# Decoder trunk on one core: the residual waits in DRAM during the experts, each pass adds its rows there, and the end works block by block

## The chip, the cores and the metric

The kernel runs on one core of a Trainium2 chip. TensorE (PE in the profile) multiplies, VectorE (DVE), ScalarE (ACT) and GpSimd (POOL) do the elementwise work, and SyncE (SP) issues most transfers. The metric is the device time of one execution in microseconds, as the median of several runs.

## The reference

Two layers over 256 tokens of width 2048, all in fp32. Each layer adds the output of an attention mixer to the residual h, and then that of a channel mixer: a dense SwiGLU in layer 0, and in layer 1 an expert SwiGLU in which each token goes to 2 of 8 experts. A final RMSNorm gives the output.

```python
h = x
for layer in range(2):
    h = h + hybrid_mixer(rmsnorm(h, attn_norm[layer]), ...)
    m = rmsnorm(h, ffn_norm[layer])
    if layer == 0:
        h = h + swiglu(m, dense_w_gate, dense_w_up, dense_w_down)
    else:
        y = 0
        for e in range(8):                       # gates are zero but for a token's top 2
            y = y + gates[:, e:e + 1] * swiglu(m, wg[e], wu[e], wd[e])
        h = h + y
return rmsnorm(h, final_norm)
```

## The kernel before

The tokens are two blocks of 128 (`BLOCKS`), which lie on the partitions; h is one tile of 128 x 2 x 2048 in on-chip memory. The 2048 columns are handled as four column blocks of 512 (`COLS`, `NCOL`). Each engine has its own program; they meet at semaphores. Weights stream through tiles of 1 MB (`raw`, `more_raw`: eight slots in the experts, issued by SP in `load` when the slot's last reader is done). A tile is two units. For each unit ACT writes the rounded part `w_hi` (`split_hi`), DVE the rest `w_lo` (`split_lo`, in the attention and dense parts one unit in four by POOL in `low_parts`), and PE multiplies hi by hi, lo by hi and hi by lo. ACT and DVE run three units ahead of PE (`LEAD`).

The experts run as passes: one pass is one expert with up to 128 of its tokens, 48 units (16 for the first half of gate and up, 16 for the second, 16 for the down product from `DOWN0` on). With these inputs there are 8 passes, of which 7 are trips of a hardware loop and the last one is written out behind it (`tail=True`). The steps around the change:

- Before the experts, DVE writes the normed token rows in four column blocks (`gained`, semaphore `n_ready`), and POOL stores them to `tokens_dram` (`rows_out`). POOL first fills spare rows of the DRAM tensor `slots_dram`, waits for that (`spare_in`), and prepares `count`, `token` and the cleared tile `x_rows`.
- PE, DVE and ACT route the tokens; DVE writes the token number of each of the 128 slots of a pass into `slot_token` (`read_slots`, `slot_ready`). POOL then gathers these rows into `x_rows`, which is the tile scr (`gather_rows`, one indirect DMA; slots without a token have a number beyond the bound and move nothing). PE transposes the rows (`turn_rows`), and the pass starts.
- In a pass ACT copies the four column blocks of the down product to `y_out` (`down_end`), and POOL stores them in three DMAs to the pass's rows of `slots_dram` (`store_y`).
- After the loop POOL gathers, for both blocks and both experts of a token, the rows of `slots_dram` at `home`, and adds them into h on the way (four indirect DMAs). It starts when a late weight tile has landed.
- The last pass's rows never go to DRAM: PE brings them back to token order with a 0/1 matrix (`put_rows`, at the units of `put_at` and once behind the pass), and DVE adds them to h (`add_back`).
- The end: DVE multiplies by the final gain (`gain_back`), ACT squares h with a row sum (`square_back`), `one_over_rms` makes the scale, DVE scales block 0 and ACT block 1, and SP stores the output.

## Time and profile before

| what | value |
|---|---|
| median of 3 runs | 2269.82 us (2269.7 to 2271.07) |
| profiled execution: span from first to last instruction | 2270.2 us |
| PE busy | 2222.1 us, 98% |
| DVE busy | 1565.4 us, 69% |
| ACT busy | 1240.7 us, 55% |
| POOL busy | 376.8 us, 17% |
| read from and written to DRAM | 515.10 MB, 15.75 MB |

The span is the only time that the profiled execution has; it lies within the range of the three runs. PE's busy time says only that matmuls follow each other closely. Times in the rows below count from the start of this span, and the experts' passes run from about 1690 to 2252.

### The profile page before, as it was taken

The page shows a single profiled execution, that of the slowest core. Times are in us where ns is not written, and L with a number is a line of the kernel's source. Part 1 is how long each engine was busy: PE and PEld are TensorE (multiplying, and loading weights), DVE is VectorE, ACT ScalarE, POOL GpSimd, SP SyncE. Part 2 cuts the span into 40 slices and gives each one's busy share as a digit, 9 for nine tenths or more (in the row PEclk, how much of TensorE's full clock was granted, in tenths as well). Part 3 has the DMA queues.
Part 4 walks back from the last instruction along what each step waited for, and adds up shares of the span by engine and source line. Part 5 has one row for each costly group of instructions (what it writes and reads, how often), then busy time and mean ns, then how long its engine had stood idle before and what let it go on. Part 6 is the DMA issues. An engine that isn't in the chain of part 4 may idle for free. (4 is left out here: it accounts for less than half of the span.)

```text
span 2270.2 us, 29218 instructions
## 1 busy us (share of the span) xinstructions
PE 2222.1 (98%) x10255; PEld 1827.3 (80%) x10255; DVE 1565.4 (69%) x1716; ACT 1240.7 (55%) x1531; POOL 376.8 (17%) x196
## 2 busy tenths in 40 slices
PE   7999999999999999999999999999999999999997
PEld 6888888888888888888877888888877888888875
DVE  4466686666655566665554466686679999999997
ACT  5445454454444344444435445454458888887885
POOL 1111221222222222222212121121210000000001
PEclk9999999999999999999999999999999999999998
DMA  7464545555565565656554454555599999999997
GB/s 245 149 191 156 185 157 190 183 172 193 180 198 186 187 200 186 193 180 198 185 177 159 153 193 149 185 173 193 185 341 349 382 383 382 381 380 374 381 383 203
DMA packets 264462, 523.43 MB, mean 231 GB/s; under 512 B 15237, under 2 KB 19465, under 8 KB 263177
## 3 DMA queue, kind: packets, MB, share of 16 engines
q1 hardware_dynamic: 259648, 500.42, 65.0%
q0 software_dynamic: 4544, 22.03, 3.0%
q8 instruction: 45, 0.74, 0.1%
q14 instruction: 25, 0.20, 0.0%
q10 hardware_dynamic: 200, 0.05, 0.0%
HBM read 515.10 MB, written 15.75 MB: 234 GB/s over the span
## 5 line engine op out<-in xcount | busy, mean ns | idle before, releaser
L660 ACT ACTIVATE w_hi<-raw 128x1024 fp32r<-128x1024 f32 x744 | 778.6, 1058 | 609.0 <-PE acc L1575 558.1
L999 DVE TENSOR_TENSOR w_lo<-raw,w_hi 128x1024 fp32r<-128x1024 f32 x606 | 758.1, 1270 | 477.1 <-ACT w_hi L660 474.9
L1573 PE MATMUL acc<-w_hi,a_hi 128*128 128x512 f32 x1632 | 644.2, 395 | 3.9 <-DVE w_lo L999 2.4
L1575 PE MATMUL acc<-w_hi,a_lo 128*128 128x512 f32 x1632 | 637.0, 390 | 0.0
L1574 PE MATMUL acc<-w_lo,a_hi 128*128 128x512 f32 x1632 | 636.6, 390 | 0.0
L572 POOL TENSOR_TENSOR w_lo<-raw,w_hi 128x1024 fp32r<-128x1024 f32 x138 | 337.8, 2447 | 1304.7 <-ACT w_hi L660 1005.2
L1573 PEld LDWEIGHTS acc<-w_hi,a_hi 128*128 128x128 f32 x1632 | 307.3, 188 | 67.7 <-DVE w_lo L999 3.8
L1575 PEld LDWEIGHTS acc<-w_hi,a_lo 128*128 128x128 f32 x1632 | 307.0, 188 | 65.1
L1574 PEld LDWEIGHTS acc<-w_lo,a_hi 128*128 128x128 f32 x1632 | 307.2, 188 | 61.4
L1866 PE MATMUL acc<-w_hi,a_hi 128*128 128x512 f32 x752 | 300.5, 400 | 4.2 <-DVE w_lo L999 4.1
L1868 PE MATMUL acc<-w_hi,a_lo 128*128 128x512 f32 x752 | 293.6, 390 | 0.0
L1867 PE MATMUL acc<-w_lo,a_hi 128*128 128x512 f32 x752 | 292.9, 389 | 0.0
L999 DVE TENSOR_TENSOR w_lo<-more_raw,w_hi 128x1024 fp32r<-128x1024 f32 x192 | 231.1, 1222 | 30.3 <-ACT w_hi L660 26.7
L1573 PE MATMUL acc<-w_hi,o_hi 128*128 128x512 f32 x608 | 240.5, 396 | 2.4 <-DVE o_lo L1282 2.4
L1575 PE MATMUL acc<-w_hi,o_lo 128*128 128x512 f32 x608 | 237.6, 391 | 0.0
L1574 PE MATMUL acc<-w_lo,o_hi 128*128 128x512 f32 x608 | 237.3, 390 | 0.0
L660 ACT ACTIVATE w_hi<-more_raw 128x1024 fp32r<-128x1024 f32 x192 | 197.5, 1054 | 21.6 <-PE acc L1868 18.0
L1866 PEld LDWEIGHTS acc<-w_hi,a_hi 128*128 128x128 f32 x752 | 141.3, 188 | 37.0 <-DVE w_lo L999 9.3
L1868 PEld LDWEIGHTS acc<-w_hi,a_lo 128*128 128x128 f32 x752 | 141.1, 188 | 30.6
L1867 PEld LDWEIGHTS acc<-w_lo,a_hi 128*128 128x128 f32 x752 | 141.4, 188 | 28.3 <-issue 0.7
L1573 PEld LDWEIGHTS acc<-w_hi,o_hi 128*128 128x128 f32 x608 | 114.6, 189 | 26.4 <-DVE o_lo L1282 2.6
L1575 PEld LDWEIGHTS acc<-w_hi,o_lo 128*128 128x128 f32 x608 | 114.6, 188 | 24.3
(237 smaller groups left out, 1497.0 us busy)
## 6 DMA issues: line engine op xcount, KB each, us to landing
raw<-in_w_in SPq DMA_DIRECT2D x112, 1024.0 KB, 5.0
raw<-in_moe_w_gate SPq DMA_DIRECT2D x64, 1024.0 KB, 10.0
more_raw<-in_moe_w_up SPq DMA_DIRECT2D x64, 1024.0 KB, 10.3
raw<-in_dense_w_gate SPq DMA_DIRECT2D x44, 1024.0 KB, 5.2
raw<-in_dense_w_up SPq DMA_DIRECT2D x44, 1024.0 KB, 5.2
raw<-in_dense_w_down SPq DMA_DIRECT2D x44, 1024.0 KB, 5.2
raw<-in_w_out SPq DMA_DIRECT2D x32, 1024.0 KB, 5.2
raw<-in_moe_w_down SPq DMA_DIRECT2D x32, 1024.0 KB, 8.2
```

Source lines behind the costliest of these rows:

```text
L572: nc.gpsimd.tensor_tensor(w_lo[:, u % SPLIT_SLOTS], raw[:, (u // TILE_UNITS) % RAW_SLOTS, u % TILE_UNITS], w_hi[:, u % SPLIT_SLOTS].bitcas ...
L660: nc.scalar.activation(w_hi[:, slot], raw_tile(tile)[1][:, u % TILE_UNITS], ACT.Copy)\
L999: nc.vector.tensor_tensor(w_lo[:, slot], raw_tile(u // TILE_UNITS)[1][:, u % TILE_UNITS], w_hi[:, slot].bitcast(F32), ALU.subtract).then_i ...
L1573: nc.tensor.matmul(dst, hi, w_hi[:, slot, c], start=first and c == 0, stop=False)
L1574: nc.tensor.matmul(dst, hi, w_lo[:, slot, c], start=False, stop=False)
L1575: ins = nc.tensor.matmul(dst, lo, w_hi[:, slot, c], start=False, stop=last and c == UNIT_CHUNKS - 1)
L1866: nc.tensor.matmul(dst, hi, w_hi[:, slot, c], start=first and c == 0, stop=False)
L1867: nc.tensor.matmul(dst, hi, w_lo[:, slot, c], start=False, stop=False)
L1868: ins = nc.tensor.matmul(dst, lo, w_hi[:, slot, c], start=False, stop=last and c == UNIT_CHUNKS - 1)
```

## The change

The residual itself is put into DRAM for the time of the experts. POOL no longer fills spare rows; behind each store of a token column block it stores the same columns of h to a new tensor `h_dram` (semaphore `h_out`). In a pass, one indirect DMA (`add_rows`) takes the place of the three stores: it adds the 128 rows of `y_out` to the rows of `h_dram` that `slot_dest` names, where slots without a token again move nothing. `slot_dest` is a copy of `slot_token` that DVE makes right before `read_slots` overwrites it, behind a wait for the add of the pass before. The four gathers after the loop and the four small DVE operations that made `home` are gone; SP loads h back in four plain DMAs, one for each column block, behind its last weight load. The end is rearranged: `put_rows` runs two units earlier for column block 1 and one unit earlier for block 2, DVE squares three of the pieces itself, adds the last column block in two halves, and folds the final gain into the scaling, so that five pieces of the output leave one after the other.

```diff
-    put_at = {DOWN0 + 9: 0, DOWN0 + 13: 1, PASS_UNITS - 1: 2}
+    put_at = {DOWN0 + 9: 0, DOWN0 + 11: 1, PASS_UNITS - 2: 2}
...
 
                     after_first(e, passes - 1)
-
-            for n, half in enumerate((slice(0, D // 2), slice(D // 2, D))):
-                for b, scaled in enumerate((r_ready, s_ready)):
-                    sp_.wait_ge(scaled, 1 + n)
-                    sp_.dma_start(out[0, b * P:(b + 1) * P, half], h_gained[:, b, half]).then_inc(stored, 16)
-            sp_.wait_ge(stored, 16 * 2 * BLOCKS)
+                    sp_.wait_ge(rows_out, lin(16 * (NCOL - 1), 16, passes))
+                    for c in range(NCOL):
+                        sp_.dma_start(h[:, :, c * COLS:(c + 1) * COLS],
+                                      h_dram[:, c * COLS:(c + 1) * COLS].rearrange("(b p) n -> p b n", p=P))\
+                            .then_inc(returned[c], 16)
+
+            for b, cols, scaled, n in OUT_PIECES:
+                sp_.wait_ge(s_ready if scaled == "act" else r_ready, n)
+                sp_.dma_start(out[0, b * P:(b + 1) * P, cols], h_gained[:, b, cols]).then_inc(stored, 16)
+            sp_.wait_ge(stored, 16 * len(OUT_PIECES))
 
 
...
-            spare = slice((EXPERTS - 1) * P, MAX_PASSES * P)
-            pool.dma_start(slots_dram[spare, :], moe_w_down[0, 0][0:(MAX_PASSES - EXPERTS + 1) * P, :]).then_inc(spare_in, 16)
-            pool.wait_ge(consts, N_CONSTS)
-            pool.dma_start(slots_dram[NO_SLOT:NO_SLOT + 1, :].rearrange("o (a n) -> (o a) n", n=P), fx_neg[0:CH, P:2 * P])\
-                .then_inc(spare_in, 16)
             pool.wait_ge(w_ready, 8 * DEPTH)
-            pool.wait_ge(spare_in, 32)
             nc.gpsimd.iota(count, pattern=[[1, P]], base=0, channel_multiplier=0,
...
@@ -593,6 +591,8 @@
                 pool.wait_ge(n_ready, q + 1)
                 pool.dma_start(tokens_dram[:, q * COLS:(q + 1) * COLS].rearrange("(b p) n -> p b n", p=P), n_rows[q])\
                     .then_inc(rows_out, 16)
+                pool.dma_start(h_dram[:, q * COLS:(q + 1) * COLS].rearrange("(b p) n -> p b n", p=P),
+                               h[:, :, q * COLS:(q + 1) * COLS]).then_inc(h_out, 16)
...
-            def y_done(jobs_, i):
+            def add_rows(i):
 
                 for s in range(2):
-                    pool.wait_ge(free[s], lin(ffn_uses[1] + jobs_[s], 4, i))
+                    pool.wait_ge(free[s], lin(ffn_uses[1] + 4, 4, i))
+                pool.wait_ge(dest_ready, lin(1, 1, i))
                 pool.sem_inc(transfer_may, 1)
-
-            def store_y(n, i, done):
-                pool.dma_start(slots_dram[bass.ds(i * P, P), Y_COLS[n]], y_out[:, Y_COLS[n]]).then_inc(done, 16)
+                pool.indirect_dma_start(h_dram[:], bass.IndirectOffsetOnAxis(slot_dest[:, 0:1], 0), y_out, None,
+                                        bounds_check=BLOCKS * P - 1, oob_is_err=False, compute_op=ALU.add)\
+                    .then_inc(rows_out, 16)
 
             gather_rows(0)
+            pool.wait_ge(h_out, 16 * NCOL)
             pool.wait_ge(table_ready, 1)
             passes = pool.value_load(table[0:1, TABLE:TABLE + 1], min_val=EXPERTS, max_val=MAX_PASSES)
             with pool.Fori(0, passes - 1) as i:
                 gather_rows(1, 1, i)
-                y_done((3, 3), i)
-                store_y(0, i, rows_out)
-                y_done((4, 3), i)
-                store_y(1, i, rows_out)
-                y_done((4, 4), i)
-                store_y(2, i, rows_out)
-            last = passes - 1
-
-            pool.wait_ge(back_ready, 1)
-            pool.wait_ge(rows_out, last * 48 + 16 * NCOL)
-
-            tile_loaded(pool, M0 // TILE_UNITS + PASS_TILES - 4, PASS_UNITS, last)
-            pool.sem_inc(transfer_may, 1)
-            for j in range(2):
-                for b in range(BLOCKS):
-                    if j:
-                        pool.wait_ge(returned[b], 16)
-                    pool.indirect_dma_start(h[:, b, :], None, slots_dram[:],
-                                            bass.IndirectOffsetOnAxis(home[:, 2 * j + b:2 * j + b + 1], 0),
-                                            compute_op=ALU.add).then_inc(returned[b], 16)
+                add_rows(i)
...
-            for c in range(NCOL):
-                square_back(c)
+            square_back(0, range(BLOCKS), 0)
+            square_back(1, range(BLOCKS), 1)
+            square_back(NCOL - 1, (1,), 2)
             norm_guess(4)
             act.wait_ge(rr_ready, 5)
-            act.wait_ge(fin_gained, NCOL)
-            for half in (slice(0, D // 2), slice(D // 2, D)):
-                nc.scalar.activation(h_gained[:, 1, half], h_gained[:, 1, half], ACT.Copy, scale=rr[:, 1:2])\
-                  .then_inc(s_ready, 1)
+            act.wait_ge(fin_gained, 1)
+            nc.scalar.activation(h_gained[:, 1, 0:2 * COLS], h_gained[:, 1, 0:2 * COLS], ACT.Copy, scale=rr[:, 1:2])\
+              .then_inc(s_ready, 1)
...
-                    dve.wait_ge(sq_cols, NCOL * n)
+                    dve.wait_ge(sq_cols, NCOL * n if n < 4 else NCOL * 3 + 3)
+                    if n == 4:
+                        dve.wait_ge(squared_own, 3)
...
-            def add_back(c):
-
-                if c == 0:
-                    for b in range(BLOCKS):
-                        dve.wait_ge(returned[b], 32)
-                dve.wait_ge(put_ps, c + 1)
-                cols = slice(c * COLS, (c + 1) * COLS)
-                nc.vector.tensor_tensor(h[:, :, cols], h[:, :, cols], put_to[c], ALU.add).then_inc(h_added, 1)
-
-            def gain_back(c):
-
-                if c == 0:
-                    dve.wait_ge(fin_in, 32)
+            def add_back(c, blocks):
+
+                if blocks[0] == 0:
+                    dve.wait_ge(returned[c], 16)
+                dve.wait_ge(put_ps, c + 1 if len(blocks) == BLOCKS else c + 1 + blocks[0])
+                cols, b0, b1 = slice(c * COLS, (c + 1) * COLS), blocks[0], blocks[-1] + 1
+                nc.vector.tensor_tensor(h[:, b0:b1, cols], h[:, b0:b1, cols], put_to[c][:, b0:b1], ALU.add)\
+                  .then_inc(h_added, 1)
+
+            def square_own(c, b, to):
+
                 dve.wait_ge(h_added, c + 1)
-                cols = slice(c * COLS, (c + 1) * COLS)
-                gain_out = fin[c // 2][:, c % 2 * COLS:(c % 2 + 1) * COLS]
-                nc.vector.tensor_tensor(h_gained[:, :, cols], h[:, :, cols],
-                                        gain_out.rearrange("p (o n) -> p o n", o=1).broadcast_to([P, BLOCKS, COLS]),
-                                        ALU.mult).then_inc(fin_gained, 1)
+                nc.vector.scalar_tensor_tensor(out=to, in0=h[:, b, c * COLS:(c + 1) * COLS], scalar=1.0,
+                                               in1=h[:, b, c * COLS:(c + 1) * COLS], op0=ALU.mult, op1=ALU.mult,
+                                               accum_out=sums[:, b, c:c + 1]).then_inc(squared_own, 1)
+
+            def gain_back():
+
+                dve.wait_ge(fin_in, 32)
+                dve.wait_ge(h_added, 2)
+                nc.vector.tensor_tensor(h_gained[:, 1, 0:2 * COLS], h[:, 1, 0:2 * COLS], fin[0], ALU.mult)\
+                  .then_inc(fin_gained, 1)
...
                 if u == slots_read and not tail:
+                    dve.wait_ge(rows_out, lin(16 * NCOL, 16, i))
+                    nc.vector.tensor_copy(slot_dest[:], slot_token[:]).then_inc(dest_ready, 1)
+                    dve.wait_ge(dest_ready, lin(1, 1, i))
                     read_slots(1, 1, i)
...
-            for c in range(NCOL):
-                add_back(c)
-                gain_back(c)
+            both = range(BLOCKS)
+            add_back(0, both)
+            add_back(1, both)
+            gain_back()
+            add_back(2, both)
+            square_own(2, 0, scr[:, 2 * COLS:3 * COLS])
+            square_own(2, 1, scr[:, 3 * COLS:4 * COLS])
+            add_back(3, (0,))
+            add_back(3, (1,))
+            square_own(3, 0, eg[:, 0])
             one_over_rms(4)
-            dve.wait_ge(fin_gained, NCOL)
-            for half in (slice(0, D // 2), slice(D // 2, D)):
-                nc.vector.tensor_scalar(h_gained[:, 0, half], h_gained[:, 0, half], rr[:, 0:1], None, ALU.mult)\
-                  .then_inc(r_ready, 1)
+            for b, cols, scaled, n in OUT_PIECES:
+                if scaled == "dve":
+                    gain_out = fin[cols.start // (2 * COLS)]
+                    at = cols.start % (2 * COLS)
+                    nc.vector.scalar_tensor_tensor(out=h_gained[:, b, cols], in0=h[:, b, cols], scalar=rr[:, b:b + 1],
+                                                   in1=gain_out[:, at:at + cols.stop - cols.start], op0=ALU.mult,
+                                                   op1=ALU.mult).then_inc(r_ready, 1)
...
                 for b in range(BLOCKS):
                     ins = nc.tensor.matmul(put_to[c][:, b], pick_any[:, b], y_out[:, c * COLS:(c + 1) * COLS], start=True, stop=True)
-                ins.then_inc(put_ps, 1)
+                    if c == NCOL - 1 or b == BLOCKS - 1:
+                        ins.then_inc(put_ps, 1)
```

POOL, from its last `low_parts` to the end of its program. Before, the two fills of `slots_dram` come first, the token stores follow each other, a pass has three stores, and the four gathers into h stand at the end:

```order
L581 DMA slots_dram<-in_moe_w_down 64x16384
L583 DMA slots_dram<-fx_neg 16x128
L587 IOTA sp 128x128
...
L594 DMA tokens_dram<-nat 128x2x512 x2
L594 DMA tokens_dram<-qT 128x2x512
L594 DMA tokens_dram<-kT 128x2x512
L606 DMA scr<-tokens_dram,slot_token 128x2048
...
L606 DMA scr<-tokens_dram,slot_token 128x2048
...
L617 DMA slots_dram<-nat 128x1024
...
L641 DMA h<-slots_dram,home 128x2048 x4
L161 UNCONDITIONAL_BRANCH
```

And of the changed kernel, the same stretch:

```order
L585 IOTA sp 128x128
...
L592 DMA tokens_dram<-nat 128x2x512
L594 DMA h_dram<-h 128x2x512
...
L592 DMA tokens_dram<-kT 128x2x512
L594 DMA h_dram<-h 128x2x512
L606 DMA scr<-tokens_dram,slot_token 128x2048
...
L606 DMA scr<-tokens_dram,slot_token 128x2048
...
L616 DMA h_dram<-nat,slot_dest 256x2048
```

The iotas and the clearing of scr now stand behind `low_parts` alone, a store of h follows each of the four stores of tokens, and one indirect DMA per pass is left beside the gather.

DVE, from the last `w_lo` of the last pass on (h is the residual, X and acc are the accumulators that `put_rows` wrote, raw is `h_gained`, sm the small sums and scales). Before:

```order
L999 TENSOR_TENSOR w_lo<-more_raw,w_hi 128x1024
L1457 TENSOR_TENSOR h<-h,X 128x2x512
L1466 TENSOR_TENSOR raw<-h,qT 128x2x512
L1457 TENSOR_TENSOR h<-h,X 128x2x512
L1466 TENSOR_TENSOR raw<-h,qT 128x2x512
L1457 TENSOR_TENSOR h<-h,acc 128x2x512
L1466 TENSOR_TENSOR raw<-h,kT 128x2x512
L1457 TENSOR_TENSOR h<-h,acc 128x2x512
L1466 TENSOR_TENSOR raw<-h,kT 128x2x512
L1036 TENSOR_REDUCE sm<-sm 128x2
L1004 TENSOR_SCALAR sm<-sm 128x2
...
L1044 TENSOR_SCALAR sm<-sm 128x2
L1558 TENSOR_SCALAR raw<-raw,sm 128x1024 x2
```

And of the changed kernel:

```order
L982 TENSOR_TENSOR w_lo<-more_raw,w_hi 128x1024
L1432 TENSOR_TENSOR h<-h,X 128x2x512 x2
L1446 TENSOR_TENSOR raw<-h,qT 128x1024
L1432 TENSOR_TENSOR h<-h,acc 128x2x512
L1438 SCALAR_TENSOR_TENSOR scr,sm<-h 128x512 x2
L1432 TENSOR_TENSOR h<-h,acc 128x512 x2
L1438 SCALAR_TENSOR_TENSOR eg,sm<-h 128x512
L1021 TENSOR_REDUCE sm<-sm 128x2
...
L1029 TENSOR_SCALAR sm<-sm 128x2
L1549 SCALAR_TENSOR_TENSOR raw<-h,sm,qT 128x512 x2
L1549 SCALAR_TENSOR_TENSOR raw<-h,sm,kT 128x1024 x2
```

Ahead of the sum stood eight operations of 1024 elements; now there are four of 1024 and five of 512, and only the last three, two adds and a square, need the last `put_rows`. The scaling has grown from two operations to four.

PE, its last rows: the last products of the pass and the products with the 0/1 matrix (`nat,wT`, each "x2" one column block). Before:

```order
L1866 MATMUL acc<-w_hi,a_hi 128x512
L1867 MATMUL acc<-w_lo,a_hi 128x512
L1868 MATMUL acc<-w_hi,a_lo 128x512
L1866 MATMUL acc<-w_hi,a_hi 128x512
L1867 MATMUL acc<-w_lo,a_hi 128x512
L1868 MATMUL acc<-w_hi,a_lo 128x512
L1855 REGISTER_ALU
L1857 MATMUL acc<-nat,wT 128x512 x4
```

And of the changed kernel, where block 2 comes ahead of the last unit (the six products) instead of behind it:

```order
L1847 REGISTER_ALU
L1849 MATMUL acc<-nat,wT 128x512 x2
L377 REGISTER_ALU
L1859 MATMUL acc<-w_hi,a_hi 128x512
L1860 MATMUL acc<-w_lo,a_hi 128x512
L1861 MATMUL acc<-w_hi,a_lo 128x512
L1859 MATMUL acc<-w_hi,a_hi 128x512
L1860 MATMUL acc<-w_lo,a_hi 128x512
L1861 MATMUL acc<-w_hi,a_lo 128x512
L1849 MATMUL acc<-nat,wT 128x512 x2
```

## Rows read from the trace of the kernel before

**Rows 1.** Stretches; us, busy of PE, PEld, DVE, ACT, POOL, PEclk, DMA share, GB/s
```profile
1666.00:1676.00 10.00, 10.00 (x50) 8.32 (x51) 9.29 (x55) 3.66 (x6) 2.35 (x4) 1.00 1.05 408
...
1770.00:1840.00 70.00, 69.57 (x320) 56.88 (x319) 66.25 (x72) 57.02 (x65) 2.73 (x4) 1.00 1.05 384
```

**Rows 2.** Timeline of POOL from 1660 on
```profile
1663.31 0.27 POOL L587 IOTA sp<- 128x128 f32 x1 [15.58 <-DMA slots_dram<-fx_neg]
...
1667.62 0.73 POOL L594 DMA_DIRECT2D tokens_dram<-kT  x1
...
1736.69 1.06 POOL L606 DMA_INDIRECT scr<-tokens_dram,slot_token  x1 [54.76 <-DVE slot_token L1411]
```

**Rows 3.** DMA issues from 1660 to 1669, last number us to landing
```profile
tokens_dram<-kT POOLq DMA_DIRECT2D x1, 512.0 KB, 11.8
```

**Rows 4.** Timeline of DVE from 1636 to 1703
```profile
1658.57 1.22 DVE L1069 TENSOR_TENSOR kT<-h,nat 128x1024 f32<-128x1024 f32 x1
...
1673.09 0.15 DVE L1411 TENSOR_SCALAR slot_token<-X 128x1 uint32<-128x1 f32 x1
```

**Rows 5.** The rows gather, tile scr
```profile
L606 POOL DMA_INDIRECT scr<-tokens_dram,slot_token x8: 1058/1091/1594, 1680.3 to 2158.1; - x8
...
DMA to landing us min/median/max: 7.1/8.2/9.8
```

**Rows 6.** Timeline of PE and chain of waits, 1679 to 1703
```profile
1687.45 1.09 PE L1848 MATMUL X<-ident,scr 128*128 128x128 f32 x8 [3.48 <-DMA scr<-tokens_dram,slot_token]
...
1692.88 0.87 PE X L1848 x8
1693.76 0.23 PE acc L1866
```

**Rows 7.** Waits of PE from 1700 to 2250
```profile
PE X L1848 <- DMA scr<-tokens_dram,slot_token: 2.4, 3, 1.7
```

**Rows 8.** DMA issues of one pass, 1770 to 1840
```profile
more_raw<-in_moe_w_up SPq DMA_DIRECT2D x8, 1024.0 KB, 10.7
```

**Rows 9.** Timelines of SP and ACT: a weight tile issued, and read
```profile
2203.09 8.37 SPq L431 DMA_DIRECT2D raw<-in_moe_w_down  x4
...
2214.22 8.68 SPq L431 DMA_DIRECT2D more_raw<-in_moe_w_down  x4
...
2220.41 1.07 ACT L660 ACTIVATE w_hi<-raw 128x1024 fp32r<-128x1024 f32 x1 [0.18 <-PE acc L1868]
```

**Rows 10.** Timeline of POOL from 2195 on
```profile
2222.05 1.76 POOL L641 DMA_INDIRECT h<-slots_dram,home  x1 [40.45 <-DMA more_raw<-in_moe_w_down]
...
2240.56 2.57 POOL L641 DMA_INDIRECT h<-slots_dram,home  x1 [2.35 <-DMA h<-slots_dram,home]
```

**Rows 11.** DMA issues from 2221 to 2224
```profile
more_raw<-in_moe_w_down SPq DMA_DIRECT2D x1, 1024.0 KB, 16.7
```

**Rows 12.** Two stretches without weight loads; last number GB/s
```profile
2240.00:2242.00 2.00, 1.00 1.00 193
...
2266.00:2268.00 2.00, 0.50 1.02 403
```

**Rows 13.** Timeline of PE from 2236 on
```profile
2246.36 1.88 PE L1857 MATMUL X<-nat,wT 128*128 128x512 f32 x4
...
2250.85 3.59 PE L1857 MATMUL acc<-nat,wT 128*128 128x512 f32 x8
```

**Rows 14.** Timelines of DVE and ACT from 2250 on
```profile
2250.73 1.22 DVE L1457 TENSOR_TENSOR h<-h,X 128x1024 f32<-128x1024 f32 x1 [4.09 <-DMA h<-slots_dram,home]
...
2260.60 0.16 DVE L1036 TENSOR_REDUCE sm<-sm 128x2 f32<-128x8 f32 x1
...
2262.49 1.41 DVE L1558 TENSOR_SCALAR raw<-raw,sm 128x1024 f32<-128x1024 f32 x2
...
2251.05 0.60 ACT L950 ACTIVATE nat<-acc 128x512 f32<-128x512 f32 x1 [5.66 <-PE acc L1868]
...
2262.62 2.19 ACT L985 ACTIVATE raw<-raw,sm 128x1024 f32<-128x1024 f32 x2 [1.29 <-DVE sm L1044]
```

More of the change, by code:

```diff
@@ L341, in trunk @@
         rows_out = sem("rows_out")
-        spare_in = sem("spare_in")
+        h_out = sem("h_out")
+        dest_ready = sem("dest_ready")
         transfer_may = sem("transfer_may")
@@ L351, in trunk @@
         gate_picked = sem("gate_picked")
-        returned = [sem(f"returned{b}") for b in range(BLOCKS)]
+        returned = [sem(f"returned{c}") for c in range(NCOL)]
         put_ready = sem("put_ready")
         put_ps = sem("put_ps")
-        back_ready = sem("back_ready")
         fin_gained = sem("fin_gained")
+        squared_own = sem("squared_own")
         s_ready = sem("s_ready")
```

30 lines of the change are left out of this document (10 added, 20 removed).

## The prediction

> **What bounds the kernel now.** I read busy time by stretch first, then who waits in the stretches that the diff touches. In a stretch of one pass's length PE is busy 69.57 of 70 us at a granted clock of 1.00 [rows 1]; in the whole of the passes its only larger waits are three, 2.4 us together, for the gather of a pass's rows [rows 7]. So the passes are bound by PE, and the change leaves PE's work in them alone. DVE is close behind, busy 66.25 of 70, and the DMA engines show a share of 1.05 at 384 GB/s: nothing there has much room [rows 1].
>
> That leaves two seams. At the start of the experts, POOL sits idle for 15.58 us until its fill of the spare rows has landed, at 1663.31 [rows 2]; only then does it store the tokens, the last one from 1667.62 to 1668.35. That store lands 11.8 us after its issue [rows 3], at 1679.4, and the gather starts 0.9 later, at 1680.3 [rows 5]. PE waits 3.48 us for it, until 1687.45, and comes back at the low clock [rows 6]. At the end, DVE waits 4.09 us for the gathers into h, until 2250.73, then works to 2260.60 before the row sums are complete, and the last scaled piece is ACT's, done at 2262.62 + 2.19 = 2264.81 [rows 14]. The span ends at 2270.2, 5.4 us later.
>
> **The first seam.** The spare fill (512 rows of 8 KB, read and written) and the wait for it go. POOL is then free for each token column block as DVE delivers it; the last is ready at 1658.57 + 1.22 = 1659.8 [rows 4], so its store is out by 1660.5, 7.8 us earlier. Even if it takes 11.8 us again it lands at 1672.3, before DVE has written the slots, at 1673.09 + 0.15 = 1673.24 [rows 4]. Now the slots release the gather. With the same 0.9 us it starts at 1674.1, and with 8.2 us to landing (7.1 to 9.8) [rows 5] the rows are there at 1682.3, at worst at 1683.9. PE is ready for them at 1687.45 - 3.48 = 1683.97. So the wait of 3.5 us is gone.
>
> The low clock goes with it. From 1687.45 to 1692.88 PE does eight transposes and one unit of twelve matmuls, 5.43 us. At the full clock, as right behind it, the eight transposes take 0.87 and a matmul 0.23 [rows 6], together 0.87 + 12 x 0.227 = 3.6 us. The idle time cost another 1.8. Gain: 3.5 + 1.8 = 5.3 us. It is between 2.2 (rival below) and 5.4; I take 5.3, since the margins on the way are 0.9 us at the slots and 0 to 2.8 at the landing.
>
> What is added here hides: the four stores of h are 2.1 MB where 8.4 MB of fill traffic leaves, they are issued by an otherwise idle POOL (0.73 us each), and the only one who waits for `h_out` is POOL behind its first gather, with its next work 50 us away (the gather at 1736.69, [rows 2]). The clearing of scr moves to about 1647, beside DVE's split work. It could hold DVE up to 1.8 us once; no row shows that pair of operations. DVE works three units ahead of PE there, some 4 us, so I take nothing.
>
> **The passes, seven times.** Three stores of 1.05 MB together go, and one indirect add comes. It moves only slots with a token: 512 token-expert pairs over 8 passes are 64 rows, 0.52 MB. The nearest row is the gather with addition at the end, which runs alone at 193 GB/s with all engines busy (share 1.00) [rows 12]; plain transfers reach 403 [rows 12] and 408 [rows 1]. So an add holds the engines 0.52 / 0.193 = 2.7 us and the stores held them 1.05 / 0.403 = 2.6: no change. The room is also there: a pass still moves 25.2 MB of weights and 0.5 MB of rows, 25.7 / 0.408 = 63 us of some 70.2, which leaves 7.2 us for the add. Its completion is wanted 40 us later (by the copy of `slot_token` at `DOWN0`, and by ACT's first `y_out`), its issue needs only POOL.
>
> What it may do is to delay weight tiles. A tile issued at 2203.09 is read by ACT at 2220.41 [rows 9], 17.3 us later, and lands within 10.7 [rows 8]: 6.6 us to spare. The tile issued together with two full gathers with addition took 16.7 [rows 11]; with a quarter of their rows in flight I expect 12 to 13. The Trainium skill (DMA: Bandwidth & Descriptors, Queues, rings and completion order) says that a semaphore increment lands only after every earlier write of that DMA engine, across its queues, so a weight tile's signal would wait for the add's writes too. The 16.7 us agree with it; by that rule alone a tile could be as late as the add itself, which here, by the rows of the gathers, would be about 10 us and inside 17.3, so it gives no other sum.
>
> DVE makes one copy more, ahead of `slot_token`: 0.15 us like its neighbour [rows 4] and a wait on itself, 0.2 to 0.25. The gather starts later by that, and PE waits for the gather already in three passes of seven [rows 7]. Cost: between 0 and 7 x 0.25 = 1.8 us; I take 0.7, three passes in full.
>
> **The end.** PE first. From its product for column block 1 at 2246.36 to that for block 2 at 2250.85 lie two units [rows 13], 12 x 0.227 = 2.7 us, so one such product costs PE 1.8. Today block 2 stands behind the last unit and hides ACT's last copy. Moved ahead of it, it puts the last unit's end from 2250.85 to 2252.6. ACT's copy starts 0.2 later and takes 0.6 [rows 14]: 2253.4. The product of block 3 then gives its first half at 2254.4 and its second at 2255.3 (3.59 us for two such products, [rows 13]).
>
> DVE was free of weights at 2250.73 - 4.09 = 2246.6. The plain loads of h replace the four gathers (2222.05 to 2250.7, [rows 10]). SP issues them behind its last weight load, at 2214.22 + 8.68 = 2222.9 [rows 9]; with at most 3 MB of weights ahead, 5.2 MB at 384 GB/s are in by 2236.5, 10 us before DVE wants them. So DVE adds blocks 0 and 1, multiplies one gain and adds block 2 (1.22 us each, [rows 14]) and squares twice (0.7 each, half as many elements) by about 2252.9. The halves of block 3 are added at 2255.0 and 2256.0, the last square ends at 2256.6. ACT squares two column blocks behind its copy (four halves of 0.67, estimated from its 0.60 copy and the read of the sum) and the last half, to 2256.9. The sums are complete at 2256.9, not 2260.60: 3.7 us earlier.
>
> The scale takes 2262.49 - 2260.60 = 1.9 us [rows 14]: 2258.8. Behind it DVE needs four two-input operations, 0.6 + 0.6 + 1.15 + 1.2 = 3.6, to 2262.4 where ACT ended at 2264.81: of the 3.7 us only 2.4 are left. The output is 2.1 MB at 403 GB/s [rows 12], 5.2 us, which before had to leave almost whole behind 2264. Now 0.8 MB can leave from 2260.2 on. If the last piece still needs 5.4 us, the gain stays 2.4; if it finds the engines free, it needs some 3.5 and the gain is 4.3. I take 4.6 for it: 2267.0, gain 3.2.
>
> **Sum.** -5.3 + 0.7 - 3.2 = -7.8, from 2270.2 to 2262.4. The median of the runs is 0.4 below the profiled span, so 2262.0.
>
> **Rivals.**
> - *The token stores stay late.* If the last one lands after 1674.8 (1683.97 - 8.2 - 0.9), PE waits again and meets the low clock. For it: each store now has a store of h in the same queue ahead of it, and weight loads run beside. Against: the fill's 8.4 MB are gone and the stores are spread over 15 us. If a third more traffic makes it 15.6 us, it lands at 1676.1: 1.3 of wait and 1.8 of clock come back, 2265.1. 12 in 100.
> - *The adds overrun the DMA engines: slower.* The add into DRAM has no row. It must read and write DRAM for each row. The 7.2 us of room hold up to 0.52 MB at 72 GB/s; each us above costs seven. At 8.3 us per add, three times my price, the gain is gone; at 9.7 the passes give 7 x 2.5 = 17.5 us back: 2279.5. PE would wait for w_lo, and w_lo for tiles. For it: 384 of 408 GB/s used, 16.7 us for a tile beside gathers. Against: 193 GB/s with addition. 12 in 100.
> - *The end does not move.* DVE's last scaling and the output remain the bound: with block 3 late by 1.8 us and squares that take longer than priced, the last piece leaves at 2264.5. 2265.0. 10 in 100.
> - *The change does not reach PE at all* (the gather late in every pass by what the seam gives). Against: the gather's price moves by 0.25 us at most. 3 in 100, near 2270.
>
> **Chances.** The forecast has 63 in 100, with its own range from 2258.5 to 2265. A change of 0.2%, 4.5 us, is about what a measurement of this kernel can tell: faster is below 2265.3. That takes the forecast and part of the first and third rival, 0.70. The rest of those and the last are the same, 0.17. Slower is 0.13. The range from 2258 to 2268 holds the forecast and the mild rivals, and leaves out the overrun.
>
> **What would show it.** Right: no wait of POOL before its iotas, a gather issued near 1674, no wait of 3.5 us on PE and no low clock near 1690; passes of the same length; h loaded before 2240; the row sums complete some 4.3 us behind PE's last unit (2252.6 to 2256.9), where it was 9.8 (2250.85 to 2260.60). Wrong: PE waits on w_lo within the first third of a pass (adds too slow), waits for the gather beyond 1 us in most passes, or an output that still takes 5.4 us behind the last scaling.

## The result, and the profile after

The changed kernel takes 2275.22 us (median of 16 runs, 2273.96 to 2276.05), the kernel before 2270.47 beside it (16 runs, 2267.45 to 2273.34): 1.002 times as long, 95% interval 1.0014 to 1.0027. It is slower by 0.2%, where I forecast 2262.0 and a range of 2258 to 2268. The profiled execution has a span of 2272.6 us and a time of 2274.41. All profiled executions behind this one have 1.6 to 1.8 us around their span too, so my "0.4 below the profiled span" was not a fixed distance, but an accident of which execution was profiled. That explains 2.2 us at most, and not the miss.

The first thing to compare is where the two traces part. The last piece of work that neither the diff nor its waits touch is POOL's last split, just ahead of its iotas. The timeline of POOL from 1640 on, of the kernel before (start us, duration):

```profile
1644.10 2.39 POOL L572 TENSOR_TENSOR w_lo<-raw,w_hi 128x1024 fp32r<-128x1024 f32 x1 [9.32 <-ACT w_hi L660]
```

And of the changed kernel, with what POOL does until the first gather:

```profile
1654.20 2.40 POOL L576 TENSOR_TENSOR w_lo<-raw,w_hi 128x1024 fp32r<-128x1024 f32 x1 [9.57 <-ACT w_hi L643]
1656.55 0.24 POOL L585 IOTA sp<- 128x128 f32 x1
...
1658.58 0.96 POOL L592 DMA_DIRECT2D tokens_dram<-nat  x1
1659.54 0.77 POOL L594 DMA_DIRECT2D h_dram<-h  x1
...
1670.19 0.72 POOL L592 DMA_DIRECT2D tokens_dram<-kT  x1 [4.66 <-DVE kT L1054]
...
1684.18 1.10 POOL L606 DMA_INDIRECT scr<-tokens_dram,slot_token  x1 [12.55 <-DVE slot_token L1396]
1741.82 1.10 POOL L606 DMA_INDIRECT scr<-tokens_dram,slot_token  x1 [56.53 <-DVE slot_token L1396]
```

The changed kernel is 10.1 us late before its first changed instruction runs. Read against that row, everything behind it went well: the iotas no longer wait ([rows 2] had 15.58 us of idle time), the gather is released by `slot_token` and no longer by the stores of tokens, and the waits of PE from 1640 to 1700 hold no gather (3.48 us in [rows 6]); the second gather is the first one in the loop.

The late part shows in PE. Groups of PE between 500 and 1160, inside layer 0's dense part, where the diff changes nothing (busy us, mean ns of one). The kernel before:

```profile
L1574 PE MATMUL acc<-w_lo,a_hi 128*128 128x512 f32 x637 | 247.8, 389 | 0.0
...
L1573 PE MATMUL acc<-w_hi,o_hi 128*128 128x512 f32 x320 | 124.5, 389 | 0.0
```

The changed kernel, same stretch:

```profile
L1566 PE MATMUL acc<-w_lo,a_hi 128*128 128x512 f32 x628 | 244.3, 389 | 0.0
L1565 PE MATMUL acc<-w_hi,o_hi 128*128 128x512 f32 x320 | 126.4, 395 | 0.0
```

The same product of the same shape takes 389 ns where the tile a_hi is its 128x128 operand, and 395 where it is o_hi. Before, both took 389. The page has 608 products with o_hi on each of the three lines, 1824 in all, and PE's busy time on it rose by 10.0 us, from 2222.1 to 2232.1.

The rest of the profile after, by the stages of the prediction. Waits of PE from 1700 on (total, times, longest):

```profile
PE acc L1859 <- DVE w_lo L982: 4.1, 10, 0.8
PE X L1840 <- DMA scr<-tokens_dram,slot_token: 2.5, 7, 0.4
PE acc L1849 <- ACT nat L933: 0.7, 1, 0.7
```

DMA issues from 1700 to 2230 (last number: median us to landing), the adds among them:

```profile
more_raw<-in_moe_w_up SPq DMA_DIRECT2D x59, 1024.0 KB, 13.5
...
h_dram<-nat,slot_dest POOLq DMA_INDIRECT x7, 12.0
```

The passes wait for the gather as much as before (2.5 us against the 2.4 of [rows 7]), only in seven small pieces. A weight tile now needs 13.5 us to land, in the same view of the kernel before 10.2; the prediction had 12 to 13, and PE's waits for w_lo did not grow with it. The end, timelines of SP, PE and DVE:

```profile
2232.80 6.46 SPq L539 DMA_DIRECT2D h<-h_dram  x4
...
2265.48 3.39 SPq L545 DMA_DIRECT2D out<-raw  x5
...
2245.03 1.88 PE L1849 MATMUL X<-nat,wT 128*128 128x512 f32 x4
...
2252.44 2.34 DVE L1432 TENSOR_TENSOR h<-h,X 128x1024 f32<-128x1024 f32 x2
...
2262.82 0.16 DVE L1021 TENSOR_REDUCE sm<-sm 128x2 f32<-128x8 f32 x1 [0.18 <-ACT scr L893]
...
2266.04 2.47 DVE L1549 SCALAR_TENSOR_TENSOR raw<-h,sm,kT 128x1024 f32<-128x1024 f32 x2
```

DVE no longer waits for h (4.09 us in [rows 14]). Since whole executions differ by more than these steps, I cut each trace at three rows that all kernels have: POOL's last split, the second gather of rows (the first one in the loop), and PE's first product that brings the last pass's rows back (`put_rows(0)`). In the changed kernel these rows stand above, in the kernel before they are at 1644.10, 1736.69 [rows 2] and, by PE's timeline:

```profile
2239.16 1.88 PE L1857 MATMUL X<-nat,wT 128*128 128x512 f32 x4
```

What lies between:

| us between | before | after | predicted change | change |
|---|---|---|---|---|
| start and POOL's last split | 1644.10 | 1654.20 | 0 | +10.1 |
| that and the second gather (first seam) | 92.59 | 87.62 | -5.3 | -5.0 |
| that and `put_rows(0)` (passes) | 502.47 | 503.21 | +0.7 | +0.7 |
| that and the end of the span | 31.04 | 27.57 | -3.2 | -3.5 |

The three steps that the change makes add up to -7.7, against -7.8 predicted. A fourth one, for which the sum had no term, is larger than all of them. How firm each row is, the other kernels of this case tell: the new end takes 27.6 or 27.7 us in every trace with it, but the passes scatter by about 2 us, so their +0.7 cannot be told from nothing.

### The profile page after: what moved, and what is told of

It reads as the page before. It is cut to its first block, busy times and chain, and to the rows that moved or that the text cites. A ratio compares the mean times of both kernels' runs of the same rounds, so it can differ in the third digit from the quotient of the medians.

```text
span 2272.6 us, 29186 instructions
## 1 busy us (share of the span) xinstructions
PE 2232.1 (98%) x10255; PEld 1825.0 (80%) x10255; DVE 1565.0 (69%) x1725; ACT 1238.2 (54%) x1524; POOL 375.3 (17%) x180
## 4 chain that ended last, share of the span: by engine, by line
PE 78%; DVE 10%; issue 5%; ACT 4%; DMA 3%; ACTq 0%; DVEq 0%; POOLq 0%; SPq 0%
PE acc L1565 20%; PE acc L1567 20%; PE acc L1566 20%; PE acc L1859 4%; PE acc L1861 4%; PE acc L1860 4%; DVE w_lo L982 3%; DMA scr<-tokens_dram,slot_token 3%; ACT w_hi L643 2%; PE X L1840 1%; PE X L1673 1%; DVE sm L987 1%; DVE nat L1125 1%; PE X L1593 0%; DVE eg L1469 0%
## 5 line engine op out<-in xcount | busy, mean ns | idle before, releaser
L643 ACT ACTIVATE w_hi<-raw 128x1024 fp32r<-128x1024 f32 x744 | 778.6, 1058 | 617.9 <-PE acc L1567 566.9
L643 ACT ACTIVATE w_hi<-more_raw 128x1024 fp32r<-128x1024 f32 x192 | 198.3, 1058 | 22.4 <-PE acc L1861 18.8
## 6 DMA issues: line engine op xcount, KB each, us to landing
raw<-in_moe_w_gate SPq DMA_DIRECT2D x64, 1024.0 KB, 13.5
more_raw<-in_moe_w_up SPq DMA_DIRECT2D x64, 1024.0 KB, 13.5
```

What stands on the lines that cost most here:

```text
L643: nc.scalar.activation(w_hi[:, slot], raw_tile(tile)[1][:, u % TILE_UNITS], ACT.Copy)\
```

## The experiments

The theory: the small tiles in front of o_hi got smaller, so o_hi, o_lo and `more_raw` moved. Every tile gets its place in a partition by its order in the program, rounded up to 32 bytes. The declarations and sizes in the kernel give the distances between the tiles, and the compiled programs the addresses: `back_at` and `home` (32 bytes each) became `slot_dest` (32), and o_hi went from byte 194176 to 194144, from a multiple of 128 to one 32 bytes short of it, while a_hi, declared earlier, stayed at 98432. The rival: the loss has another cause (the program's code, the place of DRAM buffers, the run).

### The tiles moved back, in both directions

In the pieces of code below the comments are mine, and "..." stands for lines left out.

```diff
 slot_dest = sb("slot_dest", [P, 1], U32)
+pad = sb("pad", [P, 8])                    # 32 unused bytes: o_hi at 194176
```

> The changed kernel, with an unused tile of 8 floats a partition (32 bytes) behind slot_dest, so that o_hi, o_lo and more_raw stand again at a multiple of 64 bytes in a partition, as before the change. Placement theory: the 9.8 us that the changed kernel is behind at POOL's w_lo row near 1640 us are gone (w_lo again near 1644.1), the products with o_hi take 389 ns in the mean again and not 395, and the time is 2275.2 - 9.8 = 2265.4 us, 0.998 of the kernel before, within 2263 to 2268. Rival, the loss has another cause (the shorter program, where the compiler puts the buffers in DRAM, the run itself): nothing changes, 2275 us, 1.002.

Measured: 2265.07 us (6 runs), 0.997 of the kernel before (0.9958 to 0.9982). The counterpart is the kernel before with the same line behind `home` (o_hi at 194208, 32 bytes past a multiple of 128):

> The kernel before, with the same unused 32 bytes behind home, so that o_hi, o_lo and more_raw stand 32 bytes off a multiple of 64, and nothing else is changed. Placement theory: slower by what the changed kernel is behind at 1640 us, 9 to 11 us, so 2279 to 2282, 1.004 of the kernel before, and nearly all of it ahead of 1640 us. If it is more than 11, the tiles of more_raw cost in the experts too. Rival, another cause: 2270.5 us, 1.000.

Measured: 2282.14 (5 runs), 1.0044 (1.003 to 1.0058). One unused tile takes 2275.22 - 2265.07 = 10.15 us from the one kernel and puts 2282.14 - 2271.79 = 10.35 on the other (2271.79 is the kernel before on the same chip). The first difference is between two chips; on the chip of 2265.07 the two slow kernels of the next section take 2275.75 and 2275.74. The rival is out. The products with o_hi, 500 to 1160, in the changed kernel with its tiles back and in the kernel before with its tiles moved:

```profile
L1566 PE MATMUL acc<-w_hi,o_hi 128*128 128x512 f32 x320 | 124.5, 389 | 0.0
```

```profile
L1574 PE MATMUL acc<-w_hi,o_hi 128*128 128x512 f32 x320 | 126.5, 395 | 0.0
```

Timelines of POOL and PE with the tiles back in place, the three rows of the table:

```profile
1646.01 2.39 POOL L577 TENSOR_TENSOR w_lo<-raw,w_hi 128x1024 fp32r<-128x1024 f32 x1 [9.32 <-ACT w_hi L644]
...
1733.61 1.11 POOL L607 DMA_INDIRECT scr<-tokens_dram,slot_token  x1 [56.52 <-DVE slot_token L1397]
...
2236.20 1.88 PE L1850 MATMUL X<-nat,wT 128*128 128x512 f32 x4
```

And POOL's last split in the kernel before with its tiles moved:

```profile
1655.49 2.39 POOL L573 TENSOR_TENSOR w_lo<-raw,w_hi 128x1024 fp32r<-128x1024 f32 x1 [9.57 <-ACT w_hi L661]
```

Over all kernels here, this row starts between 1643.7 and 1646.2 with o_hi at a multiple of 128 and nothing else moved (six traces, mean 1645.1), and between 1654.2 and 1655.6 with o_hi off it (five traces, mean 1655.0). That is 10.0 us for the 1783 of the 1824 products with o_hi that lie ahead of this row, 5.6 ns each.

### Another address, and only the DMA target moved back

```diff
+pad = sb("pad", [P, 16])                   # behind slot_dest: o_hi at 194208
```

> The changed kernel, with 16 unused floats (64 bytes) behind slot_dest: o_hi stands at another address, but again 32 bytes off a multiple of 64. Placement theory by multiples of 64 bytes: 2275 us as the changed kernel, o_hi products at 395 ns. Rival, any other address or size would help: 2265 us.

```diff
 o_hi, o_lo = ...                           # stay at 194144 and 210528
+pad = sb("pad", [P, 8])                    # ahead of more_raw alone: at 194176
 more_raw = sb("more_raw", [P, MOE_SLOTS - RAW_SLOTS, TILE_UNITS, UNIT_CHUNKS, COLS])
```

> The changed kernel, with the unused 32 bytes between o_hi and more_raw: o_hi and o_lo stay 32 bytes off, but the tiles of more_raw, which DMAs write to in the experts, stand at a multiple of 64 again. Theory that the products with o_hi cost it: still 2275 us, w_lo near 1654 us. Rival, the transfers into more_raw cost it: 2265 us. A side question: a tile's median landing in the passes rose from 10 to 13.5 us; if the misplaced target does it, it is back near 10 here, and if the seven adds do it, it stays at 13.5.

Measured: 2275.75 (10 runs, 1.0017) and 2275.74 (10 runs, 1.0016). Both as slow as the changed kernel: it is neither the size of the hole nor the target of the weight transfers. A few small tiles (`table`, `ncT`) move with o_hi in all these kernels and were not moved by themselves; what points at PE's operand are the rows of the products with it: at 5.6 ns each, 1824 of them are the whole loss. The side question is answered too: the landing of a tile of w_up stays at 13.5 us, so the adds cause that.

### Which operand, and which multiple

Two kernels put 32 unused bytes ahead of a pair of large tiles and 32 behind it, with o_hi and the rest meant to stay in place (both keep the 32 bytes behind `slot_dest`, so they are measured against 2265):

```diff
+pad_a = sb("pad_a", [P, 8])                # the other kernel: ahead of w_hi
 a_hi = sb("a_hi", [P, CH, BLOCKS * P], F32R)
 a_lo = sb("a_lo", [P, CH, BLOCKS * P], F32R)
+pad_b = sb("pad_b", [P, 8])                # the other kernel: behind w_lo
```

> The changed kernel with o_hi, o_lo and more_raw at a multiple of 64 bytes, but a_hi and a_lo 32 bytes off it (unused 32 bytes ahead of them and behind them). The names a_hi and a_lo are the 128x128 operand of 7152 products (1632 and 752, three of each). Theory that a loaded operand 32 bytes off makes a product 5.4 to 6 ns longer, wherever it is: 39 to 43 us slower where TensorE sets the time, so near 2305, with these products at 395 ns and not 389. In the experts, where the transfers are close to the bound too, it may be less, down to 2292. Rival, something else of o_hi's place (its address as such, or more_raw's): 2265.

> The changed kernel with all loaded operands at a multiple of 64 bytes, but w_hi and w_lo, the 512 moving columns of each product, 32 bytes off it. Theory that only the loaded operand matters: 2265. Rival, the moving operand's rows matter too, and more, since four times as many columns pass: by 6 ns for each of 8976 products 54 us slower, 2319, or more. A third: VectorE, ScalarE and POOL, which write these tiles, become slower, which would show in their rows' means and in PE's waits for w_lo.

Measured: 2305.36 us (1.0142) with a_hi and a_lo moved, 2304.23 (1.014) with w_hi and w_lo moved. The first number looks like what the theory said, but the groups of PE in that kernel, 500 to 1160, say more:

```profile
L1569 PE MATMUL acc<-w_lo,a_hi 128*128 128x512 f32 x638 | 252.3, 395 | 0.0
L1568 PE MATMUL acc<-w_hi,o_hi 128*128 128x512 f32 x292 | 115.5, 396 | 0.0
```

o_hi is slow here as well. My two holes added up to 64 bytes, so o_hi stood at 194240: a multiple of 64, but not of 128 (and in the second kernel a_hi stood like that too). So both kernels tested two things at once, and that 2305 came out is partly luck. About 10 of the 40 us belong to o_hi; a_hi's part is about 30, where the theory had 39 to 43.

The trace says where the rest is. POOL's last split starts at 1680.86 in it, 35.8 us behind the mean of the kernels in place. Less 10.0 for o_hi, that is 25.8 us for the 4800 products with a_hi ahead of it, 5.4 ns each. From the second gather to `put_rows(0)` there are some 2060 more, but this stretch takes 507.82 us, only 5.2 more than with all tiles in place (502.59), 2.5 ns for each. In place, PE waits 2.7 us for `w_lo` and 2.3 for the gather in this stretch; with the longer products it waits for neither. So a slower product costs its full price ahead of the passes, where PE hardly waits, and about half of it in this stretch, where PE has waits to give up.

The last two kernels take the two things apart:

```diff
-pad = sb("pad", [P, 8])
+pad = sb("pad", [P, 24])                   # behind slot_dest: o_hi at 194240
```

```diff
+pad_a = sb("pad_a", [P, 8])
 w_hi = sb("w_hi", [P, SPLIT_SLOTS, UNIT_CHUNKS, COLS], F32R)
 w_lo = sb("w_lo", [P, SPLIT_SLOTS, UNIT_CHUNKS, COLS], F32R)
+pad_b = sb("pad_b", [P, 24])               # 128 bytes in all: a_hi, o_hi in place
```

> The changed kernel with 24 unused floats (96 bytes) behind slot_dest: o_hi and o_lo stand at a multiple of 64 bytes that is no multiple of 128, and all other large tiles are at multiples of 128 as before. In the two kernels with a_hi or w_hi moved, o_hi stood like this, and its products too took 396 ns. Theory that the loaded operand wants a multiple of 128 bytes: slow like the changed kernel, 2275, products with o_hi at 395 ns. Rival, 64 is enough, and o_hi was slow there for another reason: 2265, 389 ns.

> The changed kernel with w_hi and w_lo, the 512 moving columns, 32 bytes off a multiple of 128, and every other large tile, a_hi and o_hi among them, at a multiple of 128. The kernel with w_hi moved had a_hi and o_hi at 64 off, so it did not tell the two apart. Theory that only the loaded operand matters: 2265, all products at 389 ns. Rival, the moving operand wants it too: by 5.4 ns for each of 8976 products up to 48 us slower, 2304 to 2313, products at 395 ns or more.

Measured: 2276.51 (10 runs, 1.002) with o_hi 64 bytes off and all else in place, and 2310.84 (4 runs, 1.0177) with only w_hi and w_lo 32 bytes off. Groups of PE, 500 to 1160, of the kernel with o_hi 64 bytes off:

```profile
L1567 PE MATMUL acc<-w_lo,a_hi 128*128 128x512 f32 x628 | 244.4, 389 | 0.0
L1566 PE MATMUL acc<-w_hi,o_hi 128*128 128x512 f32 x319 | 126.2, 396 | 0.0
```

And of the kernel with only the moving columns off:

```profile
L1569 PE MATMUL acc<-w_lo,a_hi 128*128 128x512 f32 x639 | 253.2, 396 | 0.0
...
L1568 PE MATMUL acc<-w_hi,o_hi 128*128 128x512 f32 x288 | 114.2, 397 | 0.0
```

So 64 is not enough, which also corrects the word "multiple of 64" in my earlier expectations, and my theory that only the loaded operand matters falls. The loaded operand (32, 64 or 96 bytes past a multiple of 128) or the moving one (tested at 32 only) makes the product 6 to 8 ns longer in these rows; with both off it is not twice that (2304.23 against 2310.84). The third rival is out: the rows of `w_lo` and `w_hi` are within 4 ns of those in place, and PE's waits for `w_lo` do not grow.

### The steps of the prediction, one by one

These start from the changed kernel with its tiles back in place (2265.07 us, on another chip; the kernel before takes 2271.79 there and 2271.76 here), and are read by the stretches of the table above.

**The seam put back.** POOL's fill of spare rows and of the zero row, and the wait for it:

```diff
+pool.dma_start(spare_dram[0:(MAX_PASSES - EXPERTS + 1) * P, :], moe_w_down[0, 0][0:(MAX_PASSES - EXPERTS + 1) * P, :]).then_inc(spare_in, 16)
+pool.wait_ge(consts, N_CONSTS)
+pool.dma_start(spare_dram[SPARE_ROW:SPARE_ROW + 1, :].rearrange("o (a n) -> (o a) n", n=P), fx_neg[0:CH, P:2 * P])\
+    .then_inc(spare_in, 16)
 pool.wait_ge(w_ready, 8 * DEPTH)
+pool.wait_ge(spare_in, 32)
```

> The changed kernel with its tiles back in place (the unused 32 bytes of the first experiment), and POOL's old work ahead of the experts put back: the fill of spare rows and of a zero row in DRAM, and the wait for it, ahead of the iotas. Theory that the seam gave 4.7 to 5.3 us: 2265.1 + 5 = 2270, with PE's wait of about 3.5 us for the first gather back, and the low clock after it. If the gain came only from the wait in POOL's order and another wait now ends later, less: 2267. Rival, the seam gave nothing and the gain lies elsewhere: 2265.

Measured: 2275.17 us (10 runs, 1.0015), twice the loss that I expected. Its waits of PE, 1640 to 1700, and its DMA issues, 1648 to 1675:

```profile
PE X L1849 <- DMA scr<-tokens_dram,slot_token: 8.0, 1, 8.0
```

```profile
h_dram<-h POOLq DMA_DIRECT2D x4, 512.0 KB, 12.5
...
tokens_dram<-kT POOLq DMA_DIRECT2D x1, 512.0 KB, 14.0
```

POOL issues the last token store at 1671.18 behind all others, where the kernel before did it 1667.62 - 1644.10 = 23.5 us behind its last split and this one 26.0: three of the four stores of h stand ahead of it. And that store lands after 14.0 us, not 11.8. The first gather moves back by the sum, and the wait grows from 3.5 to 8.0; from the last split to the second gather it is 97.58 us, 10.0 more than with the seam as changed. So the two edits of the seam belong together: storing h costs nothing only because the wait is gone. This is read from the rows; no kernel here has the old wait without the stores of h and otherwise the new code. PE comes back at the low clock here as well, as its row and the windows show (after the busy times: granted clock, DMA share, GB/s):

```profile
1693.35 1.97 PE L1849 MATMUL X<-ident,scr 128*128 128x128 f32 x8 [8.03 <-DMA scr<-tokens_dram,slot_token]
...
1693.00:1696.00 3.00, 2.65 (x11) 2.46 (x12) 0.71 (x2) 1.24 (x3) 0.00 (x0) 0.50 1.05 408
1696.00:1699.00 3.00, 3.00 (x17) 2.54 (x16) 1.90 (x2) 0.90 (x1) 0.00 (x0) 0.96 1.05 386
1699.00:1705.00 6.00, 6.00 (x26) 4.31 (x25) 3.83 (x5) 4.58 (x6) 0.00 (x0) 1.00 1.05 367
```

Eight transposes take 1.97 us, where the changed kernel's at 1693.92 take 1.03 in the same view. A granted clock of 0.50 is 1.2 GHz, and it is nearly back at 2.4 in the next stretch (0.96). In the kernel before, behind the shorter wait of 3.48 us, the transposes still ran at the full clock (1.09 us, granted 1.00), and only the products behind them fell to 0.50, from 1689 to 1691.

**The end put back**, the order of products, sums, gains, squares and scaling as in the kernel before, with h still loaded by SP's four plain loads:

```diff
-put_at = {DOWN0 + 9: 0, DOWN0 + 11: 1, PASS_UNITS - 2: 2}
+put_at = {DOWN0 + 9: 0, DOWN0 + 13: 1, PASS_UNITS - 1: 2}
...
+for c in range(NCOL):
+    add_back(c, both)
+    gain_back(c)
```

> The changed kernel with its tiles back in place, and the old end: puts, sums, gains, squares and scaling by whole column groups and by halves as in the kernel before, but h still comes by the new loads, issued near 2225 us. Theory that the end by block gave it: slower by 3.2 to 3.5 us, 2268.4. If the early loading of h gave a part of the 3.5 us, the old order loses less than that, 1 to 3 us: 2266 to 2268. Rival, the end gave nothing: 2265.

Measured: 2265.45 (8 runs, 0.9974). From `put_rows(0)` to the end it takes 28.69 us, where the new order takes 27.60 and the kernel before 31.04. So of the 3.4 us, 2.3 come from loading h early, and the whole rearrangement by block gives 1.1, below the 3.2 that I expected and at the low end of the milder case. The medians, 2265.45 and 2265.07 on two chips, do not tell the two orders apart. DVE with the old order:

```profile
2241.62 1.22 DVE L1432 TENSOR_TENSOR h<-h,X 128x1024 f32<-128x1024 f32 x1
...
2248.28 1.22 DVE L1432 TENSOR_TENSOR h<-h,acc 128x1024 f32<-128x1024 f32 x1 [1.73 <-PE acc L1844]
...
2253.29 0.16 DVE L1021 TENSOR_REDUCE sm<-sm 128x2 f32<-128x8 f32 x1
```

Without the wait for h, it is PE's late product that DVE waits for, and the row sums come 19.08 us behind `put_rows(0)` (2234.21 here), against 21.44 before and 17.79 by block.

**The adds as plain stores.** The rows of seven passes go to a buffer of their own and are missing from the output:

```diff
-pool.indirect_dma_start(h_dram[:], bass.IndirectOffsetOnAxis(slot_dest[:, 0:1], 0), y_out, None,
-                        bounds_check=BLOCKS * P - 1, oob_is_err=False, compute_op=ALU.add)\
-    .then_inc(rows_out, 16)
+pool.dma_start(y_dram[:], y_out).then_inc(rows_out, 16)
```

> The changed kernel with its tiles back in place, but each pass stores its rows plainly to a buffer of its own in DRAM in place of the indirect add, so that seven of the eight passes are missing from the output. The same waits stand around it. Theory of the prediction, that the adds cost the passes nothing: 2265 us, while a weight tile's median landing falls from 13.4 to about 10 us and the dip of the DMA rate at each add (316 GB/s) goes. Rival, the adds delay the weights or the gathers: faster by 0.5 to 3 us, 2262 to 2264.5.

Measured: 2262.04 (4 runs, 2259.65 to 2264.73; 0.9955, 0.9939 to 0.997). The passes take 501.60 us by its trace, against 502.59 with the adds and tiles in place. Stretches behind an add of the changed kernel (issued at 1834.20; last number GB/s), then behind a plain store (issued at 1826.64) with the landing of its kernel's tiles:

```profile
1834.00:1846.00 12.00, 12.00 (x54) 9.93 (x54) 10.81 (x10) 9.87 (x12) 2.52 (x1) 1.00 1.03 320
```

```profile
1826.00:1836.00 10.00, 10.00 (x46) 8.29 (x45) 9.18 (x9) 8.18 (x8) 0.60 (x1) 1.00 1.04 394
...
more_raw<-in_moe_w_up SPq DMA_DIRECT2D x58, 1024.0 KB, 8.4
```

The adds keep the DMA engines as busy as the stores, at 320 GB/s and not 394, and make a tile land 5 us later, and most of both is hidden. How much of it reaches the time is not settled: 1.0 us by the two traces, which is within the scatter of the passes, and 3.0 by the medians, which were taken on different chips (on the same chip, 2.4 against the next kernel and 3.4 against the one with the old end). The profiled execution is the slowest of the four, so its trace shows the least of it. The median lies in the range of the rival, at its fast end: that the adds cost nothing is not borne out.

**The copy ahead of time.** `slot_dest` is copied four units earlier in the pass, out of the way of `read_slots`:

```diff
-if u == slots_read and not tail:
+if u == slots_read - 4 and not tail:
     dve.wait_ge(rows_out, lin(16 * NCOL, 16, i))
     nc.vector.tensor_copy(slot_dest[:], slot_token[:]).then_inc(dest_ready, 1)
+if u == slots_read and not tail:
     dve.wait_ge(dest_ready, lin(1, 1, i))
```

> The changed kernel with its tiles back in place, and slot_dest copied from slot_token four units (about 10 us) earlier in a pass, ahead of the step that reads the next slots, so that VectorE does not hold the next gather back by the copy and its wait. Theory that this delay makes PE wait 0.4 us for the gather in 6 passes: the waits for it fall from 2.3 us to about 1, faster by 1 to 1.5 us, 2264. Rival, the gather is late for another reason (the 8.3 us of its own landing): no change, 2265.

Measured: 2264.48 (6 runs, 0.9968). PE's waits for the gather from 1640 on fall to 0.9 us as expected, but those for w_lo rise from 4.0 to 5.1, and the passes take 503.08 us. Waits of PE in this kernel:

```profile
PE acc L1861 <- DVE w_lo L983: 5.1, 11, 0.8
PE X L1842 <- DMA scr<-tokens_dram,slot_token: 0.9, 4, 0.3
```

What PE gains at the gather, 1.4 us, it mostly gives back at the splits, which were running close behind it. No difference that these runs can tell.

## Why the prediction was wrong

- **The step that failed** is the sum itself: "-5.3 + 0.7 - 3.2 = -7.8, from 2270.2". It starts from the old span, and so sets all work that the diff leaves alone to its old time, without a reason given. That work became 10.1 us longer, the 1824 products with o_hi at some 395 ns and not 389. No rival held this either; the one that ended slower, the overrun by the adds, did not happen. The diff shows the cause, in two lines that I read as bookkeeping: `back_at` and `home` out, `slot_dest` in. By the placement rule of the experiments, that moves each tile declared behind them by 32 bytes, and o_hi is one.
- **The first seam was right**: 5.3 predicted, 5.0 measured in both kernels (87.62 and, with tiles in place, 87.60 against 92.59). The old side is less firm: in the kernel before with its tiles moved the seam takes 94.32 us and the passes 500.49, together what they took before (594.8 against 595.1). The gather is released by the slots, PE does not wait, and eight transposes near 1694 take 1.03 us. The rival of late token stores is out: the last store lands in 7.4 us where 11.8 was assumed. What I under-rated is its "what is added here hides": it holds only beside the removal of the wait, as the 10 us of the seam put back show.
- **The passes came out near the forecast, with luck**: +0.7 in the changed kernel, +0.1 with the tiles in place. But with the same code in the passes and only tiles moved, the stretch takes 502.59 to 504.44 us (five traces), and in the kernel before 500.49 and 502.47, so 0.7 is below what it can show. The mechanism was only partly right. The copy does delay the gather (taking it away took 1.4 us of waits), but w_lo's waits replace most of it. For the adds the working had "no change". Against one plain store they cost 1.0 to 3.4 us, by the trace and the medians; against the three stores of the kernel before, whose passes take 502.47, they show no cost beyond the scatter. An add lands after 12.0 us, not about 10, and a tile after 13.4, not 12 to 13.
- **The end was right in size**: row sums 3.7 us earlier predicted, 21.44 - 17.79 = 3.65 measured; complete 4.3 us behind PE's last unit predicted, 4.35 in the trace (2262.82, the unit ending at about 2258.47); the gain 3.2 predicted, 3.5 measured. The last piece needs 4.1 us to the end, not 4.6. The rival "the end does not move" is out. The prediction did not price loading h and rearranging the end apart; the kernel with the old order shows 2.3 us for the one and 1.1 for the other. The loads also came later than forecast: with the tiles in place the last of the four is issued at 2228.9 and needs 12.1 to 12.7 us, so h is complete at about 2241, not at 2236.5. DVE first wants it at 2243.60, so this cost nothing.
- With the tiles in place the same change takes 2265.07, 0.3% faster than before: by the medians -6.7 us, by the three stretches -8.3, where I had -7.8. In these two traces the stretch ahead of them differs by 1.9 us (1646.01 against 1644.10), inside the scatter of that row, and so the spans differ by 6.4.

Open is why a 128-byte multiple matters to PE, why both operands off cost less than the moving one alone, what the moving one costs at other offsets than 32, whether other shapes and types behave the same, and the exact price of the adds. What decides the result is shown from both sides. The fastest kernels here that leave nothing out are the changed one with its tiles in place, with or without the earlier copy (2265.07 and 2264.48, no difference between them that can be told).

## What to carry to other kernels

Compare a row that the change cannot have touched before explaining anything behind it: here one row at 1644 against 1654 told more than all the seams. When a diff adds or removes even a 4-byte tile, work out where the large tiles behind it land, and keep PE's operands at a multiple of 128 bytes, by declaring the large tiles first or by a filler. And a store that is free in one order can be the longest wait in another, so undo one edit of a pair before you call the other free.

## What the runs showed of the hardware

- Products of 128x128 by 128x512 in fp32r take 389 ns (one every 0.227 us) with both operands in place, and 395 to 397 with the loaded one 32, 64 or 96 bytes past a multiple of 128, or the moving one 32 bytes past it. The weight load's own row does not show it: 188 ns either way. The Trainium skill (SBUF — State Buffer, Operand start alignment) asks for a multiple of the element size, and says that this is "about legality, not speed"; all placements here are legal by that rule, and the runs add the speed.
- VectorE and ScalarE hardly noticed: `w_lo` from `raw` took 1264 to 1270 ns with w_hi and w_lo in place and 1265 to 1266 with both 32 bytes off, `w_hi` 1058 and 1061.
- An indirect add into DRAM of 64 valid rows of 128 on average (8 KB each) lands after 12.0 us, and a weight tile (w_up) in the passes lands in 13.4 to 13.5 us beside it, against 10.2 beside the three stores of the kernel before and 8.4 beside one plain store of 1 MB.
